# Hybrid encoder trunk: the last part of the second feed-forward in two passes by tokens

## The chip, the cores and the metric

The kernel runs on one core of one Trainium2 chip. The metric is the device time of one execution in microseconds (us); the time before is the median of three runs. The profiled execution is one more run, recorded instruction by instruction. PE is TensorE (PEld its weight loads), DVE is VectorE, ACT is ScalarE, POOL is GpSimd, SP is SyncE, which here only starts transfers.

## The reference, cut to what matters

One layer: a feed-forward, a mixer, a second feed-forward, each added to the residual `x`, and a last modulated RMSNorm. There are 640 tokens: 512 prompt tokens and 128 sample tokens (8 streams of 16), 1024 features, 2816 hidden features. The end of it is

```python
    x = x + 0.5 * g3[:, None, :] * swiglu(hn, ffn_w1[l, 1], ffn_w2[l, 1])
...
shf, scf = jnp.split(sc @ w_ada_final + b_ada_final, 2, axis=-1)
y = modulate(rmsnorm(x, final_norm_g), shf, scf)    # h * (1 + scale) + shift
```

All of it is fp32. A product is made of three products of fp32r parts: high weight by high input, high by low, low by high.

## The kernel before

**Layout.** `x` stands transposed in `xT`: eight tiles of 128 features, each over `TOK` = 640 tokens (five token tiles `c` of 128; the last, `ST`, holds the samples). Outputs are wanted by tokens, so everything that leaves has to be transposed.

**Second feed-forward.** The 22 hidden tiles are done in six parts (`PARTS`); the last part has three of them. `down(fi, part, d)` multiplies the hidden tiles of a part with the block of `ffn_w2` for feature tile `d`: 3 hidden tiles by 3 fp32r products by 2 halves of 320 tokens, 18 matmuls. For the last part the first three units stand in `first_downs` in two stretches, because the last hidden tile is late. The two halves of an accumulator lie in two PSUM banks of 2 KB per partition (`acc[0]`, `acc[1]`, `pB`, `pC` have two banks each, eight in all).

**What follows a unit `d` of the last part.** DVE adds the gated sum to `xT` (`gated_samples`, `gated_prompt` twice, `add_samples`). ACT squares the tile (line 1850), DVE adds the square to `ssum` (`add_square`). ACT (`z_prompt`) and POOL (`z_samples`) scale the tile for the last norm into `tmp`, PE turns it (`z_tile`, 5 transposes of 128 x 128 into `pB`), ACT copies it to `y_row` (`z_row`). `z_tile` for tiles 0 to 5 is put between the matmuls of later units by hand (`TURNS`).

**The end.** `mean_square(4)` takes the column means of `ssum` and of the squares of the last two tiles: 15 matmuls of 128 columns, each recorded as two passes. ACT takes the root (`rms_root`), DVE the reciprocal (`r_of`). DVE then makes ten half rows (`HALF_ROWS`, 128 x 512): `y_row * rcol + shift`, and SP sends each when it is done. `shift_row` turns the shift vectors: 8 transposes for the prompt, 8 for the samples. These and the last two `z_tile` stand behind `mean_square(4)` in PE's order. `norm_samples`, `blk` and the splitting of weights into high and low parts (ACT line 1589, DVE line 2204) are shared with the rest of the kernel.

Each engine works its own list in order; semaphores join them. A `wait_ge` holds everything behind it on that engine.

Of the kernel before, what the change touches and what calls it, by code (L numbers as in the profile page):

```python
# [7 lines left out]
ACT = mybir.ActivationFunctionType  # L8
# [76 lines left out]
def trunk_program(nc, x_prompt, x_sample, state_ssm, state_conv, c_prompt, c_sample, w_ada, b_ada, norm_g,  # L85
# [249 lines left out]

    HALF_ROWS = [(h, c) for h in range(2) for c in range(ST)] + [(h, ST) for h in range(2)]
    z_bank_of = lambda f: pC if f == KD - 1 else pB
    R_TURNS = 8
    shift_rows = acc
    sh_wide = sraw[1][:, 0:D_MODEL]  # L340
# [134 lines left out]
    def slot_as(fi, b, lo):  # L475
        kind, p, j = BLOCK[b]
        if kind != "down":
            return slot_of(fi, b, lo, WB)
        return slot_of(fi, b, lo, PARTS[p] * P).rearrange("p (k n) -> p k n", n=P)

# [76 lines left out]

    LAST_SQUARE = {1: 0, 3: 1, 4: 2}
    ADDED0 = (0, 0, KD - 1, 2 * KD - 1, 3 * KD - 2)
# [293 lines left out]
    def _(pe):  # L853
# [59 lines left out]
        def mean_square(m):  # L913

            out = pC
            j = LAST_SQUARE.get(m)
            pe.wait_ge(sq_added, ADDED0[m] + KD - (j is not None) - (m == 4))
# [3 lines left out]
            if m == 4:  # L921
                pe.wait_ge(sq_ready, m * KD - 1)
                for c in range(TT):
                    mm(out[:, c * P:(c + 1) * P], rT[:, c * P:(c + 1) * P], ones_mean[:, 0:1].broadcast_to([P, P]),
                       start=False, stop=False)
# [244 lines left out]

        TURNS = {3: {12: 0}, 4: {12: 1}, 5: {6: 2}, 6: {0: 3, 12: 4}, 7: {9: 5}}

        def z_tile(f):

            pe.wait_ge(prod_ready, 3 * KD + f + 1)
            pe.wait_ge(tms_ready, 3 * KD + f + 2)
            if f == KD - 1:
                pe.wait_ge(rms_sqrt, 5)
            else:
                wait(pe, z_rowed, f)  # L1180
            for c in range(TT):
                last = nc.tensor.transpose(z_bank_of(f)[:, c * P:(c + 1) * P], tmp[f % 2][:, c * P:(c + 1) * P],
                                           ident[:, :])
            last.then_inc(z_tr, 1)

        def shift_row(kind, fs=range(KD)):

            pe.wait_ge(down_used, 2 * len(PARTS) * KD - 1 + kind)
            for f in fs:
                v = sh_wide[:, f * P:(f + 1) * P] if kind else modc[:, 9 * KD + f, 0:1].broadcast_to([P, P])  # L1190
                last = nc.tensor.transpose(shift_rows[kind][:, f * P:(f + 1) * P], v, ident[:, :])
            last.then_inc(r_tr, 1)

        def down(fi, part, d):
# [11 lines left out]
            if halves_first:  # L1206
                ks.sort(key=lambda x: x[2])
            turned = {}
            if fi == 1 and part == len(PARTS) - 1 and d > 2:
                turned = TURNS[d]  # L1210
            for j, (k, t, h) in enumerate(ks):
                if j in turned:
                    z_tile(turned[j])
                if d == 0 and t == 0 and h == 0 and k in (0, kt - 1):
# [8 lines left out]
        def ffn(fi):  # L1223

            cols = None
            for part, kh in enumerate(PARTS):
                for p in range(PART0[part], PART0[part] + kh):
# [11 lines left out]
                    if fi == 1 and p == 0:  # L1239
                        duo_cols(DUO_GAP[1])  # L1240
                        duo_cols(DUO_GAP[1] + 1)
                if cols is None:
                    first_downs(fi, part)
# [300 lines left out]
        ffn(1)  # L1544
        mean_square(4)
        pe.wait_ge(mod_ready, 6)
        shift_row(0, range(KD // 2))
        z_tile(KD - 2)
        z_tile(KD - 1)
        shift_row(0, range(KD // 2, KD))  # L1550
        shift_row(1)


    @block.scalar
    def _(act):
# [18 lines left out]
        def blk(fi, b):  # L1574
# [245 lines left out]
        def ffn(fi, squares):  # L1820

            last_part = len(PARTS) - 1
            for part, kh in enumerate(PARTS):
# [10 lines left out]
                if part == last_part:  # L1834
                    sqrt_table()
                for d in range(KD):
# [5 lines left out]
                    if fi == 1 and d > 2:  # L1842
                        for n in {3: (0,), 4: (1, 2), 5: (3,), 6: (4,), 7: (5,)}[d]:
                            z_row(n)
                    wait(act, sq_added, squares + d - fi)
                    if d == KD - 1:
                        last_square((1, 4)[fi], x0[0] + d + 1)
                        continue
                    act.wait_ge(x_ready, x0[0] + d + 1)
                    A((rT if fi == 1 and d % 2 == 0 else sq)[:, :], tile(xT, d), ACT.Square).then_inc(sq_ready, 1)  # L1850
                    if fi == 1:
                        if d == 0:
                            act.wait_ge(mod_ready, 6)
                        z_prompt(d)
            x0[0] += KD
# [233 lines left out]
        ffn(1, ADDED0[4])  # L2089
        rms_root(4)  # L2090
        z_row(KD - 2)
        z_row(KD - 1)


    @block.vector
    def _(dve):
# [389 lines left out]
        def down(fi, part, d, q, between):  # L2486
# [6 lines left out]
            if last and d == KD - 1:  # L2493
                add_gated_by_halves((1, 4)[fi], a, q, (blk_done, b + 1), used, between)
                return
# [9 lines left out]
            else:  # L2505
                st.done(ins)

        def ffn(fi, q, sq0):

            cols = None  # L2510
            for part, kh in enumerate(PARTS):
# [15 lines left out]
                if part == len(PARTS) - 1:  # L2527
                    dve.wait_ge(ssum_zero, 1 + 2 * fi)
                for d in range(KD):
                    down(fi, part, d, q, lambda: add_square(sq0 + KD - 2 - fi, sq))  # L2530
                    if part == len(PARTS) - 1 and fi == 1:
                        if d == KD - 1:
                            dve.wait_ge(x_ready, 2 * KD + d + 1)
                            dve.wait_ge(z_tr, d - 1)
                            V.tensor_scalar(out=tmp[d % 2][:, 0:SEQ], in0=xT[:, d * TOK:d * TOK + SEQ],
                                            scalar1=modc[:, 10 * KD + d, 0:1], scalar2=None, op0=ALU.mult
                                            ).then_inc(prod_ready, 1)
                    if part == len(PARTS) - 1 and 0 < d < KD - 1:
                        if fi == 0:
                            add_square(sq0 + d - 1)  # L2540
                        elif d < KD - 2:
                            add_square(sq0 + d - 1, (rT, sq)[(d - 1) % 2])
                    for n in LOWS_BESIDE[d] if third_beside(fi, part) else (d,):
# [353 lines left out]
        ffn(1, 2, 3 * KD)  # L2897
        r_of(4)
        dve.wait_ge(rcol_ready, 5)

        def rows(c, a, b):
            return V.scalar_tensor_tensor(out=y_row[:, c, a:b], in0=y_row[:, c, a:b], scalar=rcol[:, c:c + 1],
                                          in1=shift_rows[int(c == ST)][:, a:b], op0=ALU.mult, op1=ALU.add)
        for n, (h, c) in enumerate(HALF_ROWS):
            if n == 0:
                dve.wait_ge(r_tr, R_TURNS + 1)
                dve.wait_ge(z_rowed, KD // 2)
            if n == ST:
                dve.wait_ge(r_tr, R_TURNS + 2)
                dve.wait_ge(z_rowed, KD)  # L2910
            if n == 2 * ST:
                dve.wait_ge(r_tr, R_TURNS + 3)
            rows(c, h * BANK, (h + 1) * BANK).then_inc(row_done, 1)

# [29 lines left out]
```

## Time and profile before

| | us |
|---|---|
| median of 3 runs (range) | 1439.24 (1438.28 to 1440.54) |
| time of the profiled execution | 1438.4 |
| its span, first to last instruction | 1436.8 |
| PE busy | 1419.7 (99%) |
| DVE busy | 1027.4 (72%) |
| ACT busy | 669.3 (47%) |
| POOL busy | 64.9 (5%) |

The span is what the trace covers; the run's time is 1.6 us longer. Matmuls are pipelined: one of 320 columns is recorded with some 309 ns, but starts 147 ns after the one before it. So a length of PE work is counted by starts, not by the durations of single instructions. In a timeline a line with `x5` is five instructions in a row, and its second number their common length.

### The profile page before, as it was taken

Reading aid. Unit: us, or ns where it says so; the run is one execution under the profiler, and the core shown is the slowest. Engines: PE = TensorE matmul, PEld = TensorE weight load, DVE = VectorE, ACT = ScalarE, POOL = GpSimd, SP = SyncE. Lnnn points to the kernel's source line nnn. Section 1 sums busy time; section 2 is a strip of 40 time slices with the busy share of each in tenths; the row PEclk is TensorE's granted clock in tenths of the full one; section 3 lists DMA queues with packets and bytes.
Section 4 is the critical chain, followed back from the end, with each engine's and each line's share of the span. In section 5 each row is a group of like instructions: output and inputs, shape, how many; then the busy total and the mean of one; then the engine's idle time right before and its main releaser. Section 6 shows DMA issues by size and latency. Waiting matters only on the chain.

```text
span 1436.8 us, 25703 instructions
## 1 busy us (share of the span) xinstructions
PE 1419.7 (99%) x10190; PEld 1367.3 (95%) x10190; DVE 1027.4 (72%) x1770; ACT 669.3 (47%) x1204; POOL 64.9 (5%) x109
## 2 busy tenths in 40 slices
PE   8999999999999999999999999999999999999997
PEld 6899999999999899998789999998999999999997
DVE  5887677676776776667876667557977686767776
ACT  5644425253435453666835453226525253534354
POOL 2000000000000130000100000004000000000001
PEclk9999999999999999999999999999999999999999
DMA  9752524444344612241352222443324222231222
GB/s 323 220 180 60 190 75 148 118 147 147 110 140 132 185 33 71 74 107 46 113 168 79 76 63 72 132 141 112 118 60 147 60 88 89 85 92 52 82 74 74
DMA packets 219565, 161.03 MB, mean 112 GB/s; under 512 B 6858, under 2 KB 204678, under 8 KB 219458
## 3 DMA queue, kind: packets, MB, share of 16 engines
q1 hardware_dynamic: 217490, 153.89, 36.0%
q0 software_dynamic: 1696, 5.56, 1.3%
q8 instruction: 74, 1.21, 0.4%
q14 instruction: 33, 0.27, 0.1%
q10 hardware_dynamic: 272, 0.10, 0.0%
HBM read 151.50 MB, written 8.03 MB: 111 GB/s over the span
## 4 chain that ended last, share of the span: by engine, by line
PE 93%; DVE 4%; POOL 1%; ACT 1%; DMA 1%; issue 1%; SPq 0%; DVEq 0%; ACTq 0%
PE acc L869 25%; PE pC L1098 19%; PE acc L1216 19%; PE acc L1098 15%; PE acc L1165 2%; PE pB L1014 2%; PE acc L1084 1%; PE pC L1356 1%; PE acc L1065 1%; PE pB L950 1%; PE pC L957 1%; PE pC L1491 1%; DMA x_row<-in_x_sample 1%; PE pB L1341 1%; PE acc L886 0%
## 5 line engine op out<-in xcount | busy, mean ns | idle before, releaser
L1589 ACT ACTIVATE slot<-raw 128x512 fp32r<-128x512 f32 (+1 forms) x312 | 191.0, 616 | 238.5 <-PE acc L1216 136.3
L2204 DVE TENSOR_TENSOR slot<-raw,slot 128x512 fp32r<-128x512 f32 (+1 forms) x312 | 210.3, 676 | 50.5 <-ACT slot L1589 48.1
L1216 PE MATMUL acc<-hid_hi,slot 128*128 128x320 f32 x1240 | 238.4, 310 | 0.0
L1098 PE MATMUL pC<-hn_hi,slot 128*128 128x320 f32 x960 | 227.7, 310 | 0.0
L1216 PEld LDWEIGHTS acc<-hid_hi,slot 128*128 128x128 f32 x1240 | 195.1, 188 | 2.9 <-issue 1.6
L1098 PEld LDWEIGHTS pC<-hn_hi,slot 128*128 128x128 f32 x960 | 164.4, 188 | 2.9 <-issue 2.9
L869 PE MATMUL acc<-hn_hi,whi 128*128 128x320 f32 x672 | 161.0, 321 | 0.0
L1098 PE MATMUL acc<-tT,slot 128*128 128x320 f32 x960 | 154.2, 309 | 0.3 <-DVE slot L2204 0.3
L869 PE MATMUL acc<-hn_hi,wlo 128*128 128x320 f32 x672 | 153.1, 309 | 0.0
L869 PE MATMUL acc<-hn_lo,whi 128*128 128x320 f32 x672 | 152.9, 309 | 0.0
L1098 PE MATMUL pC<-hn_lo,slot 128*128 128x320 f32 x480 | 148.2, 309 | 0.0
L1098 PEld LDWEIGHTS acc<-tT,slot 128*128 128x128 f32 x960 | 143.7, 188 | 0.6 <-DVE slot L2204 0.6
L1216 PE MATMUL acc<-hid_lo,slot 128*128 128x320 f32 x620 | 142.0, 308 | 0.0
L869 PEld LDWEIGHTS acc<-hn_hi,whi 128*128 128x128 f32 x672 | 111.8, 188 | 6.3 <-issue 5.9
L869 PEld LDWEIGHTS acc<-hn_lo,whi 128*128 128x128 f32 x672 | 112.3, 188 | 0.0
L869 PEld LDWEIGHTS acc<-hn_hi,wlo 128*128 128x128 f32 x672 | 112.2, 188 | 0.0
L1216 PEld LDWEIGHTS acc<-hid_lo,slot 128*128 128x128 f32 x620 | 103.8, 188 | 0.0
L2136 DVE TENSOR_TENSOR xadd<-acc,gate 128x128 f32<-128x128 f32 x95 | 27.6, 290 | 90.1 <-PE acc L1216 76.2
L1098 PEld LDWEIGHTS pC<-hn_lo,slot 128*128 128x128 f32 x480 | 90.1, 188 | 0.0
L2106 DVE TENSOR_TENSOR wlo<-wraw,whi 128x1024 fp32r<-128x1024 f32 x50 | 61.0, 1221 | 38.5 <-ACT whi L1569 38.0
L2130 DVE SCALAR_TENSOR_TENSOR xT<-acc,gate,xT 128x320 f32<-128x320 f32 (+1 forms) x190 | 82.6, 475 | 0.2 <-PE acc L886 0.2
L1098 PE MATMUL pC<-tT,slot 128*128 128x320 f32 x480 | 76.9, 308 | 0.0
(396 smaller groups left out, 2366.9 us busy)
## 6 DMA issues: line engine op xcount, KB each, us to landing
raw<-in_ffn_w SPq DMA_DIRECT2D x86, 512.0 KB, 5.1
sraw<-in_w_ada SPq DMA_DIRECT2D x26, 1024.0 KB, 7.6
wraw<-in_w_in SPq DMA_DIRECT2D x36, 512.0 KB, 3.8
raw<-in_ffn_w SPq DMA_DIRECT2D x16, 1024.0 KB, 5.0
ada_raw<-in_w_ada SPq DMA_DIRECT2D x8, 1024.0 KB, 11.2
wraw<-in_w_out SPq DMA_DIRECT2D x16, 512.0 KB, 4.2
raw<-in_ffn_w SPq DMA_DIRECT2D x8, 768.0 KB, 4.4
sraw<-in_w_ada_final SPq DMA_DIRECT2D x6, 1024.0 KB, 7.3
```

Source lines behind the costliest of these rows:

```text
L869: last = mm(acc[p][:, h * BANK:h * BANK + HALF], w[:, k, :], a[:, k * TOK + h * HALF:k * TOK + (h + 1) * HALF], start=(k == 0 and t == 0), ...
L950: last = nc.tensor.transpose(out[:, c * P:(c + 1) * P], src[:, c * P:(c + 1) * P], ident[:, :])
L957: last = mm(ch_rows[bank][q * QUAD:(q + 1) * QUAD, :], c_f32[:, k, :], kxn(raw, KD, ADA_COLS)[:, k, :], start=(k < P // QUAD), stop=(k >= ...
L1014: last = mm(q_rows[lane_of(duo)][q * QUAD:(q + 1) * QUAD, :], c_f32[:, k, :], kxn(duo_raw(duo, j), KD, ADA_COLS)[:, k, :], start=(kk == 0) ...
L1098: last = mm(out, w[:, kk * P:(kk + 1) * P], a, start=(first and kk == 0 and t == 0), stop=(kk == KQ - 1 and t == 2), skip_group_check=not ...
L1165: last = mm(a[h], w[t // 2][:, k, :], (hid_hi, hid_lo)[t % 2][:, k * TOK + h * HALF:k * TOK + (h + 1) * HALF], start=(k == 0 and t == 0), ...
L1216: last = mm(a[h], w[t // 2][:, k, :], (hid_hi, hid_lo)[t % 2][:, k * TOK + h * HALF:k * TOK + (h + 1) * HALF], start=(k == 0 and t == 0), ...
L1589: A(slot_as(fi, b, 0), source_of(fi, b), ACT.Copy).then_inc(blk_hi, 1)
L2106: V.tensor_tensor(out=weights(n, i, 1, w), in0=wraw[p][:, 0:w], in1=weights(n, i, 0, w).bitcast(F32), op=ALU.subtract).then_inc(wlo_done, 1)
L2130: return V.scalar_tensor_tensor(out=x[:, s:e], in0=a[s // HALF][:, p:p + e - s], scalar=gate[:, q, f * GRP:f * GRP + 1], in1=x[:, s:e], op ...
L2136: V.tensor_tensor(out=by_stream(xadd[:, SEQ:TOK]), in0=by_stream(a[1][:, SEQ - HALF:HALF]), in1=g, op=ALU.mult)
L2204: V.tensor_tensor(out=slot_as(fi, b, 1), in0=source_of(fi, b), in1=slot_as(fi, b, 0).bitcast(F32), op=ALU.subtract).then_inc(blk_lo, 1)
```

## The change

The last part of the second feed-forward gets functions of its own, `last_downs`, on PE, ACT and DVE. Tokens are worked in two passes.

- **Late pass**: tokens 256 to 639 (two prompt tiles and the samples, 384 columns) for all eight `d`, 9 matmuls of 384 columns each, every `d` in a bank of its own (`LATE_BANK`). For `d` 0 to 4 the first two hidden tiles are done for all five units, then the last hidden tile.
- **Early pass**: tokens 0 to 255 (256 columns), 9 matmuls each, two banks in turn (`EARLY_BANK`). The same weight blocks are used a second time, so the block of `d` = 7 gets a place in `hn_lo`.
- `ssum` is only added up for the late tokens. For the early tokens PE takes the column means of each unit's squares at once (`early_sum`), adding in PSUM (`sum_bank`).
- The transposes are 3 per tile for the late and 2 for the early tokens, all into one bank, `z_bank_out`.
- The root of the late tokens is taken after the late pass, the six half rows of token tiles 2, 3 and `ST` are made by DVE between the early units, and four half rows are left for the end.
- Both `shift_row` calls move ahead, into the passes.

In the order of PE (`zL`, `zE` are the transposes of late and early tokens, `sE` is `early_sum`):

```
late 0-4 (two hidden tiles), late 0-4 (last one), late 5, zL0, late 6, zL1, zL2, late 7, zL3,
early 0, zL4, early 1, zL5, zL6, shift 0, zL7, early 2, late_sums, shift 1, early 3, early 4,
zE0, sE0, zE1, sE1, early 5, zE2, sE2, early 6, zE3, sE3, zE4, sE4, early 7, zE5, sE5, zE6, sE6, sE7, zE7
```

The core of the diff:

```diff
+    SPLIT = 2 * P
+    LATE = ST - 1
+    LATE_ROWS = [(h, c) for c in (2, 3, ST) for h in range(2)]
+    HALF_ROWS = LATE_ROWS + [(h, c) for h in range(2) for c in range(2)]
+    banks = [t[:, i * BANK:(i + 1) * BANK] for t in (acc[0], acc[1], pB, pC) for i in range(2)]
+    LATE_BANK = (2, 3, 4, 5, 6, 1, 0, 7)
+    EARLY_BANK = (4, 5)
+    z_bank_out, sum_bank = banks[2], banks[3]
...
 # PE
+        def late_z(f):
+            pe.wait_ge(prod_ready, 3 * KD + f + 1)
+            pe.wait_ge(tms_ready, 3 * KD + f + 2)
...
+            wait(pe, z_rowed, f)
+            for i in range(LATE):
+                last = nc.tensor.transpose(z_bank_out[:, i * P:(i + 1) * P], tmp[f % 2][:, SPLIT + i * P:SPLIT + (i + 1) * P],
                                            ident[:, :])
             last.then_inc(z_tr, 1)
+        def early_z(f):
+            pe.wait_ge(prod_ready, 4 * KD + f + 1)
+            pe.wait_ge(z_rowed, KD + f)
+            for i in range(2):
+                last = nc.tensor.transpose(z_bank_out[:, i * P:(i + 1) * P], tmp[f % 2][:, i * P:(i + 1) * P], ident[:, :])
+            last.then_inc(z_tr, 1)
+        def early_sum(d):
+            if d == 0:
+                pe.wait_ge(rms_sqrt, 5)
+            pe.wait_ge(sq_ready, 4 * KD + d + 1)
+            for i in range(2):
+                last = mm(sum_bank[:, i * P:(i + 1) * P], (rT, sq)[d % 2][:, i * P:(i + 1) * P],
+                          ones_mean[:, 0:1].broadcast_to([P, P]), start=(d == 0 and i == 0), stop=(d == KD - 1 and i == 1))
+            last.then_inc(rms_mm if d == KD - 1 else sqhalf_ready, 1)
...
 # ACT
+        def early_row(f):
+            act.wait_ge(z_tr, KD + f + 1)
+            A(y_row[:, 0:2, f * P:(f + 1) * P], z_bank_out[:, 0:SPLIT].rearrange("p (c n) -> p c n", c=2), ACT.Copy
               ).then_inc(z_rowed, 1)
+        def early_square(d):
+            act.wait_ge(x_ready, 3 * KD + d + 1)
+            if d >= 2:
+                act.wait_ge(sqhalf_ready, len(LAST_SQUARE) + d - 1)
+            A((rT, sq)[d % 2][:, 0:SPLIT], xT[:, d * TOK:d * TOK + SPLIT], ACT.Square).then_inc(sq_ready, 1)
+        def last_downs():
+            blk(1, NB - 1)
+            act.wait_ge(mod_ready, 6)
+            for d in range(KD):
+                late_square(d)
+                if d >= 2:
+                    late_row(d - 2)
+                late_prompt(d)
+            late_row(6)
+            early_square(0)
+            early_prompt(0)
+            late_row(7)
+            early_square(1)
+            early_prompt(1)
+            token_root(LATE, 2, 4)
+            for d in range(2, KD):
+                early_square(d)
+                early_row(d - 2)
+                early_prompt(d)
+            early_row(6)
+            token_root(2, 0, 5)
+            early_row(7)
...
 # DVE
+            for d in range(KD):
+                a, x = banks[EARLY_BANK[d % 2]], tile(xT, d)
+                dve.wait_ge(x_ready, 3 * KD + d)
+                dve.wait_ge(half_done, len(LAST_SQUARE) + d + 1)
+                V.scalar_tensor_tensor(out=x[:, 0:SPLIT], in0=a[:, 0:SPLIT], scalar=gate[:, q, d * GRP:d * GRP + 1],
+                                       in1=x[:, 0:SPLIT], op0=ALU.mult, op1=ALU.add).then_inc(x_ready, 1)
+                if d == 3:
+                    token_r(2, LATE, 5)
+                    dve.wait_ge(r_tr, R_TURNS + 2)
+                    dve.wait_ge(z_rowed, KD)
+                if 3 <= d < 6:
+                    rows_of(LATE_ROWS[2 * (d - 3):2 * (d - 2)])
+            token_r(0, 2, 6)
+            dve.wait_ge(z_rowed, KD + KD // 2)
+            rows_of(HALF_ROWS[6:8])
+            dve.wait_ge(z_rowed, 2 * KD)
+            rows_of(HALF_ROWS[8:10])
```

## Rows read from the trace of the kernel before

**Rows 1.** The page: busy time of PE and DVE, share of the span.

```profile
PE 1419.7 (99%) x10190; PEld 1367.3 (95%) x10190; DVE 1027.4 (72%) x1770; ACT 669.3 (47%) x1204; POOL 64.9 (5%) x109
```

**Rows 2.** The chain that ended last, its end: start, length, what.

```profile
1398.48 3.52 PE acc L1165 x24
...
1425.26 1.13 PE pC L932 x10
...
1426.42 0.28 ACT rcol L1593
...
1426.72 0.20 DVE rcol L2216
```

**Rows 3.** Busy time by stretch: PE, PEld, DVE, ACT, POOL, granted clock, DMA.

```profile
1398.30:1426.20 27.90, 27.90 (x206) 27.67 (x205) 18.49 (x43) 17.72 (x28) 5.55 (x8) 1.00 0.00 1
```

**Rows 4.** Timeline, first unit and one set of transposes: start, length.

```profile
1398.32 0.45 PE L1165 MATMUL acc<-hid_hi,slot 128*128 128x320 f32 x2
...
1427.20 0.71 PE L1182 MATMUL pC<-ident,tmp 128*128 128x128 f32 x5
```

**Rows 5.** Groups by shape in one stretch of 1.3 us, and its timeline.

```profile
L1341 PE MATMUL pB<-wd,after_r 128*128 128x512 f32 x4 | 1.1, 394 | 0.0
646.18 1.09 PE L1341 MATMUL pB<-wd,after_r 128*128 128x512 f32 x4
```

**Rows 6.** Timeline of the end: ACT, DVE and their predecessors on PE.

```profile
1426.65 0.71 PE L1182 MATMUL pB<-ident,tmp 128*128 128x128 f32 x5
1426.94 6.67 DVE L2902 SCALAR_TENSOR_TENSOR y_row<-y_row,rcol,acc 128x512 f32<-128x512 f32 x10
1427.40 0.70 ACT L1613 ACTIVATE y_row<-pB 128x640 f32<-128x640 f32 x1 [0.71 <-PE pB L1182]
...
1428.00 0.70 ACT L1613 ACTIVATE y_row<-pC 128x640 f32<-128x640 f32 x1
```

**Rows 7.** Groups by shape, 1370 to 1440: busy, mean ns, idle before.

```profile
L2902 DVE SCALAR_TENSOR_TENSOR y_row<-y_row,rcol,acc 128x512 f32<-128x512 f32 x10 | 6.7, 741 | 0.0
L1850 ACT ACTIVATE rT<-xT 128x640 f32<-128x640 f32 x4 | 3.0, 739 | 3.4 <-DVE xT L2140 3.4
L1815 ACT ACTIVATE tmp<-pC 128x320 f32<-128x320 f32 x3 | 1.3, 438 | 2.2 <-PE pC L1098 2.2
L1620 ACT ACTIVATE sq<-xT 128x320 f32<-128x320 f32 x1 | 0.5, 470 | 0.3 <-DVE xT L2140 0.3
```

**Rows 8.** Timeline of another `mean_square`, where PE waits for a square of ACT.

```profile
976.67 0.53 PEld L932 LDWEIGHTS pC<-ones_mean,sq 128*128 128x128 f32 x4
976.78 1.52 PE L932 MATMUL pC<-ones_mean,sq 128*128 128x128 f32 x10
976.84 0.47 ACT L1620 ACTIVATE sq<-xT 128x320 f32<-128x320 f32 x1 [3.44 <-DVE xT L2140]
977.36 0.74 PEld L932 LDWEIGHTS pC<-ones_mean,sq 128*128 128x128 f32 x6 [0.17 <-ACT sq L1620]
```

**Rows 9.** Timeline of DVE in one unit of the last part.

```profile
1413.03 0.29 DVE L2136 TENSOR_TENSOR xadd<-acc,gate 128x128 f32<-128x128 f32 x1 [1.13 <-PE acc L1216]
1413.24 0.87 DVE L2130 SCALAR_TENSOR_TENSOR xT<-acc,gate,xT 128x320 f32<-128x320 f32 x2
...
1414.35 0.82 DVE L2212 TENSOR_TENSOR ssum<-ssum,sq 128x640 f32<-128x640 f32 x1
```

**Rows 10.** Busy time by stretch, as rows 3: the very end, and a busy mixed stretch.

```profile
1429.00:1430.00 1.00, 0.22 (x3) 0.00 (x0) 1.00 (x3) 0.00 (x0) 0.00 (x0) 1.00 1.03 379
...
1432.00:1433.00 1.00, 0.00 (x0) 0.00 (x0) 1.00 (x3) 0.00 (x0) 0.00 (x0) 0.50 1.03 381
716.00:720.00 4.00, 3.22 (x32) 1.53 (x28) 3.15 (x5) 2.46 (x3) 1.04 (x2) 1.00 1.01 309
```

**Rows 11.** Issues of the output transfers: count, KB, median us to landing.

```profile
out_y_prompt<-y_row SPq DMA_DIRECT2D x8, 256.0 KB, 2.2
out_y_sample<-y_row SPq DMA_DIRECT2D x2, 256.0 KB, 2.5
```

More of the change, by code:

```diff
@@ L1169, in first_downs @@
                         last.then_inc(blk_done, 1)
[L1171 to L1173 removed]
+        def late_z(f):
             pe.wait_ge(prod_ready, 3 * KD + f + 1)
             pe.wait_ge(tms_ready, 3 * KD + f + 2)
[L1177 to L1182, printed above, removed]
+            if f == 0:
+                pe.wait_ge(down_used, (2 * len(PARTS) - 1) * KD + LATE_BANK.index(2) + 1)
+            wait(pe, z_rowed, f)
+            for i in range(LATE):
+                last = nc.tensor.transpose(z_bank_out[:, i * P:(i + 1) * P], tmp[f % 2][:, SPLIT + i * P:SPLIT + (i + 1) * P],
@@ new lines, in late_sums @@
+        def late_sums():
+            pe.wait_ge(sq_added, ADDED0[4] + KD - 1)
+            for i in range(LATE):
+                mm(sum_bank[:, i * P:(i + 1) * P], ssum[:, (2 + i) * P:(3 + i) * P],
+                   ones_mean[:, 0:1].broadcast_to([P, P]), start=(i == 0), stop=False)
+            pe.wait_ge(sq_ready, 4 * KD)
+            for i in range(LATE):
+                last = mm(sum_bank[:, i * P:(i + 1) * P], sq[:, (2 + i) * P:(3 + i) * P],
+                          ones_mean[:, 0:1].broadcast_to([P, P]), start=False, stop=(i == LATE - 1))
+            last.then_inc(rms_mm, 1)
@@ new lines, in early_sum, with shift_row @@
+        def early_sum(d):
[6 more added lines that the diff above has]
+            last.then_inc(rms_mm if d == KD - 1 else sqhalf_ready, 1)
+        def shift_row(kind):
+            for f in range(KD):
@@ L1207, in down @@
                 ks.sort(key=lambda x: x[2])
[L1208 to L1213, printed above, removed]
+            for k, t, h in ks:
                 if d == 0 and t == 0 and h == 0 and k in (0, kt - 1):
@@ L1241, in ffn @@
                         duo_cols(DUO_GAP[1] + 1)
+                if fi == 1 and part == len(PARTS) - 1:
+                    last_downs()
+                    continue
                 if cols is None:
@@ L1614, in z_row, with late_square, early_prompt @@
               ).then_inc(z_rowed, 1)
+        def late_square(d):
+            wait(act, sq_added, ADDED0[4] + d - 1)
+            act.wait_ge(x_ready, 2 * KD + d + 1)
+            A((rT, sq)[d % 2][:, SPLIT:TOK], xT[:, d * TOK + SPLIT:(d + 1) * TOK], ACT.Square).then_inc(sq_ready, 1)
+        def early_prompt(f):
+            if f >= 2:
+                act.wait_ge(z_tr, KD + f - 1)
+            A(tmp[f % 2][:, 0:SPLIT], xT[:, f * TOK:f * TOK + SPLIT], ACT.Copy, scale=modc[:, 10 * KD + f, 0:1]
+              ).then_inc(prod_ready, 1)
@@ L1835, in ffn @@
                     sqrt_table()
+                if part == last_part and fi == 1:
+                    last_downs()
+                    continue
                 for d in range(KD):
@@ L2506, in down, with part_square, rows @@
                 st.done(ins)
+        def part_square(k, square, a, b, added):
+            dve.wait_ge(sq_ready, k + 1)
+            dve.wait_ge(sq_added, ADDED0[4] + added)
+            V.tensor_tensor(out=ssum[:, a:b], in0=ssum[:, a:b], in1=square[:, a:b], op=ALU.add).then_inc(sq_added, 1)
+        def rows(c, a, b):
+            return V.scalar_tensor_tensor(out=y_row[:, c, a:b], in0=y_row[:, c, a:b], scalar=rcol[:, c:c + 1],
+                                          in1=shift_rows[int(c == ST)][:, a:b], op0=ALU.mult, op1=ALU.add)
@@ L2897, in _ @@
         ffn(1, 2, 3 * KD)
[L2898 to L2913, printed above, removed]
     top.close()
```

166 lines of the change are left out of this document (117 added, 49 removed).

## The prediction

> **What bounds the kernel now.** I read the page first: PE is busy for 99% of the span [rows 1], so time can be won only by taking work off PE, or at the end, where PE has stopped. Second, the stretches: from the first matmul of the last part (1398.32 [rows 4]) to the last sum PE is busy for 27.90 of 27.90 us [rows 3]. Third, the chain that ended last: it is PE up to the sums, then the root on ACT at 1426.42, the reciprocal at 1426.72 [rows 2], and from 1426.94 the ten half rows on DVE, 6.67 us [rows 6], then the last transfer. So the end has three pieces: PE 27.9 us, then 0.20 to the root and 0.52 from root to first row, then rows of 6.67 us to 1433.6, and 3.2 us from there to 1436.8. The change shortens the third piece; the question is what it puts into the first.
>
> **Durations by start.** 24 matmuls of 320 columns take 3.52 us in the chain [rows 2]: 0.1467 each. Four of 512 columns last 1.09 us in all and one alone 0.394 [rows 5]: (1.09 - 0.394) / 3 = 0.232 from start to start. A line through both gives 0.175 for 384 columns and 0.118 for 256. Five transposes begin at 1426.65 and the next five at 1427.20 [rows 4, 6]: 0.110 each. Ten passes of the sums take 1.13 us [rows 2], near 0.111 each when not held.
>
> **PE's work up to the last sum.** Before: 144 products x 0.1467 = 21.1; 30 transposes (tiles 0 to 5) = 3.3; 15 sums in two passes, 30 x 0.111 = 3.3. Together 27.7; the trace has 27.9. After: the products are the same columns, 72 x 0.175 + 72 x 0.118 = 21.1, no change. But now stand ahead of the last sum 38 transposes of tiles (24 late, 14 early) and all 16 of the shift vectors, 54 x 0.110 = 5.9, and 22 sums (6 in `late_sums`, 16 in the `early_sum`s), 44 x 0.111 = 4.9. Together 31.9: 4.0 us more, with no wait counted. That is the price of the moves: tiles 6 and 7 and the shift vectors stood behind the sums and were hidden under the rows of DVE; now they delay the sums. Not adding up the early squares costs PE 7 more sums and takes eight additions of 256 columns off DVE, which is idle a third of the stretch (18.49 busy of 27.90 [rows 3]): it gives nothing.
>
> **The price of 256 columns.** No row has an fp32r product so narrow. It can't be shorter than a pass of the sums, which also loads 128 x 128 weights: 0.111. It can't be longer than at 320 columns, 0.147, if loading sets the pace. Against 0.118 that is -0.5 and +2.1 us over 72 products. I take 0.118, since the 320 and 512 column rows lie near a proportion to columns, and keep both ends. The Trainium skill ("TensorE: Matmul & The Clock Gate", LDWEIGHTS) has a load cost by its weight columns alone, some 107 ns for 128, and a product 2.5 ns over its columns at 2.4 GHz, 109 ns here: by that rule the split, which loads all weights twice, comes just short of being bound by loads, and the sum would be 0.65 us lower. No row here shows it.
>
> **The waits that come in.** All transposes go into one bank, `z_bank_out`. Set f+1 may start only when ACT has copied set f to `y_row`. How long PE then stands:
> - From the last transpose to the start of ACT's copy: 1427.20 to 1427.40, 0.20 [rows 4, 6].
> - The copy from PSUM lasts 438 ns for 320 columns [rows 7] and 0.70 us for 640 [rows 6], so 0.49 for 384 and 0.39 for 256.
> - From an end on ACT to PE in flow again: the square ends at 976.84 + 0.47 = 977.31, the loads resume at 977.36 [rows 8], and a matmul follows its load by 0.11 (976.67 to 976.78): 0.16.
>
> Late pass: where two sets stand with nothing between (zL1 to zL2, zL5 to zL6) PE stands 0.20 + 0.49 + 0.16 = 0.85. Twice: 1.7 us. Elsewhere an early or late unit (1.06 or 1.58) or 8 transposes (0.88) cover it.
>
> Early pass: ACT's list is square(d), copy(d-2), prompt(d). Square(d) of d >= 2 waits until `early_sum(d-2)` has read the buffer that it writes. So the copy which frees the bank is queued behind a square that waits for the sum which PE does after the transposes. From the end of a sum: 0.20, the square of 256 columns, the copy 0.39, and 0.16. The square lasts 470 ns at 320 columns and 739 at 640 [rows 7], so 0.41 at 256; the next instruction starts some 0.1 before its end (copies of 0.70 start 0.60 apart [rows 6]), so 0.32. Sum 1.07. Where an early unit stands between, its 9 x 0.118 = 1.06 covers it, for the matmul needs no more than the semaphore then (0.96). Where none stands, PE waits: zE0 sE0 to zE1, zE3 sE3 to zE4, zE5 sE5 to zE6. Three times 1.07 = 3.2 us.
>
> What is queued behind each wait is all of PE: the next sums, the next unit, and the last sum. Together 4.9 us of standing. DVE's late units are not the bound: one takes 1.32 us to the start of its `ssum` addition with 0.87 of it in two gated additions [rows 9]; with one of 256 columns (some 0.48) and `ssum` at 384 (0.55, overlapping 0.09) it is 1.39. Eight from 1404.35 give the last `x` at 1415.1 and its square at 1415.7; copy 5 on ACT waits for its transposes until 1416.0 anyway. The margin is 0.3, so a DVE unit longer by 0.2 would cost some 1.0. The square, copy and prompt of ACT take 1.26 in that 1.39. POOL's tile, the `d` = 7 block in `hn_lo` (both parts ready before unit 7, at 1411) and the waits for banks (four of them are free, as each late `d` has its own) cost nothing; the six late rows (4.0 us) on DVE lie between units where DVE would idle, and each early unit's own addition waits less than a row.
>
> **The end.** After the last sum: 0.20 + 0.52 as before, then four rows. Rows start (6.67 - 0.74) / 9 = 0.66 apart: 3 x 0.66 + 0.74 = 2.7 in place of 6.67, a gain of 4.0. The piece from the last row to the end: the transfers run at 379 GB/s with the DMA engines full from 1429 [rows 10], and the last two land after 2.5 us where the others need 2.2 [rows 11]. With six rows sent earlier this queue is shorter: I take 0.2 off (none to 0.4).
>
> **The sum.** PE 27.9 becomes 31.9 + 4.9 = 36.8: +8.9. Rows -4.0, tail -0.2. Together +4.75: a span of 1441.6 against 1436.8. The profiled execution took 1438.4, 0.8 below the median of three; I add the difference to the median: 1439.24 + 4.75 = 1444.0.
>
> **Rivals.** 0.2% of the time, 2.9 us, is about what a measurement of this kernel tells from no change.
> - *The forecast*: chance 0.52. For it: the waits follow from the order of the lists, each piece has a row. Against: copies and hand-overs of these widths aren't in the trace.
> - *Not slower: PE's stops are mostly hidden.* One mechanism: the copy is out before the square it is queued behind matters, because the sum ends earlier than I lay out. If only 0.20 + 0.39 + 0.16 less the 0.44 of the sum remains, an early stop is 0.31, three save 2.3, and the time is 1441.7; with the late stops covered too, 1440.0. It decides from 1.9 us of the 4.9 on. Against it: `early_square` names the sum as its release, and ACT works in order. Chance 0.23, of which 0.05 for faster by over 0.2%, which needs a still shorter tail and shorter sums besides.
> - *Weight loads bind at 256 columns*: 0.147 each, +2.1, 1446.1. For it: PEld is busy for 27.67 of 27.90 us [rows 3]. Against: the sums' passes load as much in 0.111. Chance 0.12.
> - *DVE binds the late pass*, as POOL and ACT run beside it: +1.0, 1445.0. Chance 0.09.
> - *The granted clock falls* to its lower level, 1.2 GHz, in the early pass. At the end it is 1.00 in 1429 to 1430, where PE stops, and 0.50 in 1432 to 1433 [rows 10]; but in a stretch with PE at 3.22 of 4.00 us it stays 1.00, and the stops here are near 1 us each. If it fell from early unit 5 on, some 7 us of PE work would double: 1451. Chance 0.04. The same page of the Trainium skill (Part 4) says that transposes don't count as busy for the clock; the 54 here stand between products, and rows 10 don't bear that out.
>
> **The numbers.** Slower by over 0.2%: 0.52 + 0.12 + 0.09 + 0.04 = 0.77. Within: 0.18. Faster: 0.05. The range takes the narrow product's upper end and half of the hidden-stop case: 1440.6 to 1446.6. The likeliest case's own range is 1442.7 to 1445.3 (five stops known to 0.1 or 0.2 each, 256 columns at 0.111 to 0.125).
>
> **What the profile after would show.** PE standing after zE0 sE0, zE3 sE3 and zE5 sE5 for about 1 us, ended by ACT's copy into `y_row`; after zL1 and zL5 for 0.85; no other stop of over 0.3. Products of 256 columns 0.118 apart. The last sum near 1435.1, 8.9 later than before. Four rows after it, 2.7 us. Wrong would be: stops under 0.4 in the early pass, which takes 2 us off, products at 0.147, or DVE ending the late pass.

## The result, and the profile after

The changed kernel takes 1444.17 us (median of 12 runs, 1442.68 to 1445.21), the kernel before 1440.47 us in its 12 runs (1438.28 to 1442.83). The ratio is 1.0028, with a 95% interval of 1.0021 to 1.0035: slower, by 3.0 to 5.0 us, with 4.0 in the middle (the two medians are 3.70 apart). The forecast was slower by 4.75 us.

The profiled execution took 1443.73 us, its span is 1442.1. The page: the busy line that answers to [rows 1], and the output transfers that answer to [rows 11].

```profile
PE 1422.7 (99%) x10204; PEld 1368.9 (95%) x10204; DVE 1025.8 (71%) x1771; ACT 673.3 (47%) x1229; POOL 63.1 (4%) x109
...
out_y_prompt<-y_row SPq DMA_DIRECT2D x8, 256.0 KB, 2.3
out_y_sample<-y_row SPq DMA_DIRECT2D x2, 256.0 KB, 2.1
```

Busy time by stretch, columns as in [rows 3]: from the first product to the end of the last sum, and two stretches of 1 us at the very end.

```profile
1399.00:1436.17 37.17, 33.04 (x244) 31.88 (x243) 21.04 (x50) 22.89 (x54) 3.84 (x8) 1.00 0.12 44
1440.00:1441.00 1.00, 0.00 (x0) 0.00 (x0) 0.00 (x0) 0.00 (x0) 0.00 (x0) 0.50 1.04 387
1441.00:1442.00 1.00, 0.00 (x0) 0.00 (x0) 0.00 (x0) 0.00 (x0) 0.00 (x0) 0.50 0.24 88
```

PE was busy for 27.90 of 27.90 us before [rows 3]. Now the stretch is 37.17 us long and PE is busy for 33.04 of it. So both terms are there: more work, and some 4 us in which nothing runs. The recorded end of a matmul lies behind the start of the next one, so the first 0.16 us of each stop still count as busy. Counted by starts, as the forecast did it, PE stands for 4.96 us and works for 32.2. The granted clock is 1.00 throughout.

The timeline shows where PE stands. Columns: start, length, engine, line, what; in brackets the idle time before, and who ended it. That idle time runs from the recorded end, so it is 0.16 or 0.17 us shorter than the stand counted by starts, which the text gives unless it says otherwise.

```profile
1399.04 0.33 PE L1233 MATMUL acc<-hid_hi,slot 128*128 128x384 f32 x1
...
1410.35 0.49 PE L1182 MATMUL acc<-ident,tmp 128*128 128x128 f32 x3
...
1410.87 0.49 ACT L1711 ACTIVATE y_row<-acc 128x384 f32<-128x384 f32 x1
1410.98 0.40 POOL L852 TENSOR_TENSOR tmp<-xT,modc 128x128 f32<-128x128 f32 x1 [1.38 <-PE acc L1182]
...
1411.51 0.52 PE L1182 MATMUL acc<-ident,tmp 128*128 128x128 f32 x3 [0.67 <-POOL tmp L852]
...
1417.38 0.52 PE L1182 MATMUL acc<-ident,tmp 128*128 128x128 f32 x3 [0.67 <-POOL tmp L852]
...
1424.19 1.41 DVE L2662 SCALAR_TENSOR_TENSOR y_row<-y_row,rcol,acc 128x512 f32<-128x512 f32 x2
...
1424.34 0.38 PE L1191 MATMUL acc<-ident,tmp 128*128 128x128 f32 x2
...
1424.56 0.61 PE L1212 MATMUL acc<-ones_mean,rT 128*128 128x128 f32 x4
...
1425.27 0.42 ACT L1738 ACTIVATE rT<-xT 128x256 f32<-128x256 f32 x1 [3.44 <-PE acc L1212]
1425.51 0.48 DVE L2697 SCALAR_TENSOR_TENSOR xT<-pB,gate,xT 128x256 f32<-128x256 f32 x1
1425.59 0.36 ACT L1730 ACTIVATE y_row<-acc 128x256 f32<-128x256 f32 x1
...
1426.10 0.41 PE L1191 MATMUL acc<-ident,tmp 128*128 128x128 f32 x2 [0.93 <-ACT y_row L1730]
...
1431.46 0.41 PE L1191 MATMUL acc<-ident,tmp 128*128 128x128 f32 x2 [0.93 <-ACT y_row L1730]
...
1435.04 0.41 PE L1191 MATMUL acc<-ident,tmp 128*128 128x128 f32 x2 [0.93 <-ACT y_row L1730]
...
1435.73 0.61 PE L1212 MATMUL acc<-ones_mean,sq 128*128 128x128 f32 x4
...
1436.38 0.26 ACT L1743 ACTIVATE rcol<-acc,eps_t 128x2 f32<-128x2 f32 x1 [0.51 <-PE acc L1212]
...
1436.87 2.72 DVE L2662 SCALAR_TENSOR_TENSOR y_row<-y_row,rcol,acc 128x512 f32<-128x512 f32 x4
```

**Early stops.** The four passes of `early_sum(0)` begin at 1424.56 and take 4 x 0.111, to 1425.00; zE1 begins at 1426.10. That is a stand of 1.10. In between, in ACT's order: the square from 1425.27, and behind it the copy from 1425.59, which ends at 1425.95 and lets PE go on 0.15 later. The pieces are 0.27 + 0.32 + 0.36 + 0.15, where the forecast had 0.20 + 0.32 + 0.39 + 0.16. It happens three times, ahead of zE1, zE4 and zE6.

**Late stops.** zL1 begins at 1410.35 and takes 3 x 0.11, to 1410.68; zL2 begins at 1411.51: 0.83, and once more before zL6. Here the profile names POOL as the one who ended it. But the POOL instruction at 1410.98 is a tile that PE doesn't need yet. ACT's copy, which ends at 1410.87 + 0.49 = 1411.36, fits with its hand-over of 0.15. The experiment with a bank more settles it.

The chain that ended last runs through all three early stops; a part of it, with the last one:

```profile
1432.32 1.06 PE pB L1233 x9
...
1434.20 0.42 ACT sq L1738
1434.62 0.28 ACT y_row L1730
```

Its first line also has the price that no row of before showed: nine products of 256 columns in 1.06 us, 0.118 each.

**Count from the first product.** No code ahead of the last part differs, and yet the first product of the last part begins at 1398.32 before [rows 4] and at 1399.04 after, and anywhere from 1397.87 to 1401.95 in the profiles below. So two profiles are compared from that product on, and what a kernel is worth is taken from the ratios.

| | before | after | difference | forecast |
|---|---|---|---|---|
| first product to root | 28.10 | 37.34 | +9.24 | +8.9 |
| root to end of span | 10.38 | 5.72 | -4.66 | -4.2 |
| together | 38.48 | 43.06 | +4.58 | +4.75 |

### The profile page after: what moved, and what is told of

Its sections match the earlier page's. It is cut to its first block, busy times and chain, and to the rows that moved or that the text cites. A ratio compares the mean times of both kernels' runs of the same rounds, so it can differ in the third digit from the quotient of the medians.

```text
span 1442.1 us, 25783 instructions
## 1 busy us (share of the span) xinstructions
PE 1422.7 (99%) x10204; PEld 1368.9 (95%) x10204; DVE 1025.8 (71%) x1771; ACT 673.3 (47%) x1229; POOL 63.1 (4%) x109
## 4 chain that ended last, share of the span: by engine, by line
PE 92%; DVE 3%; ACT 1%; SPq 1%; POOL 1%; DMA 1%; issue 1%; DVEq 0%; POOLq 0%; ACTq 0%
PE acc L877 25%; PE pC L1101 19%; PE acc L1316 18%; PE acc L1101 15%; PE pB L1017 2%; PE acc L1168 2%; PE acc L1087 1%; PE pC L1459 1%; DMA ada_raw<-in_w_ada 1%; PE pB L1233 1%; PE acc L1068 1%; PE pB L953 1%; PE pC L1594 1%; PE pB L1444 1%; PE acc L894 0%
## 5 line engine op out<-in xcount | busy, mean ns | idle before, releaser
L1316 PE MATMUL acc<-hid_hi,slot 128*128 128x320 f32 x1180 | 225.2, 309 | 0.0
L1316 PEld LDWEIGHTS acc<-hid_hi,slot 128*128 128x128 f32 x1180 | 185.4, 188 | 2.9 <-issue 2.1
L1316 PE MATMUL acc<-hid_lo,slot 128*128 128x320 f32 x590 | 134.7, 308 | 0.0
L1316 PEld LDWEIGHTS acc<-hid_lo,slot 128*128 128x128 f32 x590 | 98.7, 188 | 0.0
L1101 PE MATMUL acc<-hn_hi,slot 128*128 128x320 f32 x320 | 76.9, 309 | 0.0
```

The costliest lines, as they stand in the source:

```text
L1101: last = mm(out, w[:, kk * P:(kk + 1) * P], a, start=(first and kk == 0 and t == 0), stop=(kk == KQ - 1 and t == 2), skip_group_check=not ...
L1316: last = mm(a[h], w[t // 2][:, k, :], (hid_hi, hid_lo)[t % 2][:, k * TOK + h * HALF:k * TOK + (h + 1) * HALF], start=(k == 0 and t == 0), ...
```

## Experiments

"To root" is from the first product of the last part to the root of the last tokens, from the profile. Each ratio is to runs of the kernel before on the same chip, side by side with the kernel's own.

| kernel | ratio to before | 95% interval | to root | to end |
|---|---|---|---|---|
| changed kernel | 1.0028 | 1.0021 to 1.0035 | 37.34 | 43.06 |
| copy first | 1.0014 | 1.0005 to 1.0023 | 34.66 | 40.39 |
| early bank | 1.0007 | 0.9998 to 1.0016 | 34.76 | 40.49 |
| late bank | 1.0020 | 1.0011 to 1.0029 | 36.19 | 41.95 |
| both banks | 1.0003 | 0.9994 to 1.0012 | 33.46 | 39.16 |
| sum alone | 1.0012 | 1.0003 to 1.0021 | 35.01 | 40.75 |
| both banks, DVE sums | 1.0002 | 0.9993 to 1.0011 | 33.17 | 38.88 |
| combined | 0.9992 | 0.9983 to 1.0001 | 31.82 | 37.57 |
| before, work moved | 1.0008 | 0.9999 to 1.0017 | 29.52 | 40.61 |
| rows first | 0.9975 | 0.9964 to 0.9985 | 30.14 | 35.83 |
| rows first, sums at once | 0.9996 | 0.9987 to 1.0005 | 32.81 | 38.52 |

**1. The copy ahead of the square on ACT (e1_copy_first).** It tests the claimed cause of the early stops by order alone.

```diff
             for d in range(2, KD):
+                early_row(d - 2)
                 early_square(d)
-                early_row(d - 2)
                 early_prompt(d)
```

> Edit: in ACT's early list the copy into y_row of tile d-2 stands before the square of d instead of behind it. Theory (PE's three early stops of 1.10 us are the chain sum, square, copy): a stop becomes 0.20 + 0.37 + 0.16 less the 0.44 of the sum, about 0.3 us; three save 2.3 us, span about 1439.8 against 1442.1 of the changed kernel, ratio to before about 1.0012. Rival (the stops are set by the scaled tile or the buffers of the squares, and the copy only happens to be last): the stop stays over 0.9 us and the span within 0.5 of 1442.1.

Measured 1442.29 us, ratio 1.0014. The timeline at the place of the first early stop:

```profile
1426.23 0.61 PE L1212 MATMUL acc<-ones_mean,rT 128*128 128x128 f32 x4
1426.43 0.38 ACT L1730 ACTIVATE y_row<-acc 128x256 f32<-128x256 f32 x1 [2.93 <-PE acc L1191]
...
1426.93 0.42 ACT L1738 ACTIVATE rT<-xT 128x256 f32<-128x256 f32 x1
1426.96 0.41 PE L1191 MATMUL acc<-ident,tmp 128*128 128x128 f32 x2
```

The copy now runs while PE takes the sums, and the stand is 1426.96 - 1426.67 = 0.29 in place of 1.10. The other two are 0.29 as well. Three times 0.81 is 2.4; the root comes 2.7 us sooner. The cause is shown: the stop is the square that waits for the sum and has the copy behind it.

**2. A second bank for the early transposes (e2_early_bank).** The same stops, taken on from PE's side. Odd tiles go to the bank that holds half of the samples' shift vectors, so the samples' late rows are made first. The transposes and ACT's copy then use `early_out(f)`.

```diff
-    LATE_ROWS = [(h, c) for c in (2, 3, ST) for h in range(2)]
+    LATE_ROWS = [(h, c) for c in (ST, 2, 3) for h in range(2)]
...
+    early_out = lambda f: banks[(2, 6)[f % 2]]
...
-            pe.wait_ge(z_rowed, KD + f)
+            pe.wait_ge(z_rowed, KD + max(f - 1, 0))
+            if f == 1:
+                pe.wait_ge(row_done, 2)
```

> Edit: the early transposes go into two PSUM banks in turn (bank 2 and the first of pC, free after the samples' rows, which DVE makes first), so set f+1 waits for the copy of set f-1. Theory: the stop before the second set stays at 0.7 us (it waits for the samples' rows), the two others vanish; the last sum comes 2.3 to 2.5 us earlier, span about 1439.7, ratio to before about 1.0012. Rival (the square waiting for the sum is what counts, not the bank): PE stops for as long before the next sum instead, span within 0.5 of 1442.1.

Measured 1441.19 us, ratio 1.0007, somewhat under the expectation. The root comes 2.6 us sooner. One early stop is left, a new one of 0.73 (0.57 in the bracket): PE waits for DVE's first two rows to free the bank. The expectation had 0.7 for it.

```profile
1427.20 0.41 PE L1194 MATMUL pC<-ident,tmp 128*128 128x128 f32 x2 [0.57 <-DVE y_row L2665]
```

**3. A second bank for the late transposes (e3_late_bank).** It decides who ends the late stops.

```diff
+    late_out = lambda f: banks[2 + f % 2]
...
-            wait(pe, z_rowed, f)
+            wait(pe, z_rowed, f - 1)
...
         def late_sums():
 
+            pe.wait_ge(z_rowed, KD)
```

> Edit: the late transposes go into two banks in turn (bank 3 is free until the late sums). Theory (the two late stops of 0.83 us are PE waiting for ACT's copy out of the one bank): zL1-zL2 has no stop, zL5-zL6 one of 0.3 us because ACT then scales tile 6 just in time; 1.25 us less, span about 1440.85, ratio to before about 1.0020. Rival (POOL's scaling of the samples, which the profile names as releaser, binds): both stops stay at 0.8, span 1442.1.

Measured 1442.28 us, ratio 1.0020. The timeline, around zL1 and zL2, and around zL5 and zL6:

```profile
1409.65 0.82 PE L1185 MATMUL acc<-ident,tmp 128*128 128x128 f32 x6
...
1410.23 0.42 PE L1237 MATMUL pC<-hid_hi,hn_lo 128*128 128x384 f32 x1
...
1410.29 0.41 POOL L853 TENSOR_TENSOR tmp<-xT,modc 128x128 f32<-128x128 f32 x1 [1.38 <-PE acc L1185]
...
1414.67 1.05 PE L1185 MATMUL acc<-ident,tmp 128*128 128x128 f32 x6
1415.56 1.04 PE L1224 MATMUL acc<-ident,modc 128*128 128x128 f32 x8
```

Six transposes stand in a row. POOL's instruction begins at 1410.29, when the product behind them has already started, so POOL released none of them; in the changed kernel it was the copy. The two stops were 1.66 us; the root comes 1.15 sooner, since the second pair takes 0.89 where 6 x 0.11 would do, and there are gaps of some 0.1 before zL7 and in `late_sums`.

**4. Both banks (e4_both_banks).** Both edits together: do they add up?

> Edit: e2 and e3 together. Theory: the savings add, 3.5 us, PE stands for about 1.5 us of the 5.0 in all, span about 1438.6, ratio to before about 1.0004 (within 0.2% of before): the change without its stops is then no gain, since the longer PE work ahead of the last sum (4 us) uses up the four rows' worth that the end gives back. Rival (the stops are only a part and other losses show up): span above 1440.

Measured 1440.69 us, ratio 1.0003. The root comes 3.88 us sooner than in the changed kernel; the edits alone gave 2.58 and 1.15. They add up: 3.73, and 3.88 measured. But the kernel is only even with the one before: what is left is the added work of PE against the rows saved. One stop of over 0.3 us is left, of 0.73:

```profile
1423.65 0.41 PE L1197 MATMUL pC<-ident,tmp 128*128 128x128 f32 x2 [0.57 <-DVE y_row L2669]
```

**5. The sums at once undone alone (e8_sum_alone).** DVE adds up the early squares 0 to 5; PE takes means of `ssum` and of squares 6 and 7. All else is as in the changed kernel.

```diff
+            if d < KD - 2:
+                return
+            if d == KD - 2:
...
+                    mm(sum_bank[:, i * P:(i + 1) * P], ssum[:, i * P:(i + 1) * P],
+                       ones_mean[:, 0:1].broadcast_to([P, P]), start=(i == 0), stop=False)
...
-                act.wait_ge(sqhalf_ready, len(LAST_SQUARE) + d - 1)
+                act.wait_ge(sq_added, ADDED0[4] + LATE_ADDED + d - 1)
...
+                if 0 < d < KD - 1:
+                    part_square(4 * KD + d - 1, (rT, sq)[(d - 1) % 2], 0, SPLIT, LATE_ADDED + d - 1)
```

> The changed kernel with one part undone: the early squares 0 to 5 are added up by DVE and TensorE takes 12 passes in place of 32. Everything else, the single bank for transposes and the order of ACT's list included, stays. My account: 2.2 us less TensorE work ahead of the root; the square of d + 2 now waits for DVE's addition and no longer for TensorE's sum, but the copy that frees the bank is still queued behind it, so three early stops of about 0.9 to 1.4 each stay or grow because the passes of the sums between sets of transposes no longer cover part of them: root 36 us after the first product instead of 37.3, ratio to the kernel before 1.0017 to 1.0022. Rival (the sums at once were the main cost of the change): ratio 1.0012 or less, root at 35.1 or earlier.

Measured 1441.53 us, ratio 1.0012, root at 35.01: the rival's numbers, not mine. I had expected the stops to grow by some 0.9 us (2.2 of work saved, and the root only 1.3 sooner). The timeline:

```profile
1428.21 0.41 PE L1192 MATMUL acc<-ident,tmp 128*128 128x128 f32 x2 [0.56 <-ACT y_row L1738]
...
1432.15 0.41 PE L1192 MATMUL acc<-ident,tmp 128*128 128x128 f32 x2 [1.04 <-ACT y_row L1738]
...
1433.37 0.42 ACT L1746 ACTIVATE rT<-xT 128x256 f32<-128x256 f32 x1 [0.96 <-DVE xT L2705]
...
1434.20 0.41 PE L1192 MATMUL acc<-ident,tmp 128*128 128x128 f32 x2 [0.61 <-ACT y_row L1738]
...
1435.17 0.41 PE L1192 MATMUL acc<-ident,tmp 128*128 128x128 f32 x2 [0.57 <-ACT y_row L1738]
```

Four stands of 0.73, 1.19, 0.77 and 0.75 (from the end of the transposes or products before) make 3.44 in place of 3.30. The saving stays whole: 20 passes x 0.111 = 2.2, of 2.33 measured. The copy no longer waits for a sum of PE, only for DVE and the square. Taking the column means at once is the largest single piece of work that the change put in PE's way, at 2.2 us; the five stops together cost more than twice that.

**6. Both banks and the sum by DVE (e5_dve_sum).** The edit of 5 on the kernel of 4.

> The kernel with a bank more for both kinds of transposes (the kernel of the run before this one), and the early squares of units 0 to 5 are added up by DVE again; TensorE takes the column means of that sum and of the squares 6 and 7 only: 12 passes instead of 32, so 20 x 0.111 = 2.2 us less TensorE work ahead of the root. Theory A (the sums that stand in the way are a plain cost of TensorE): the root comes 2.2 us earlier, 31.3 us after the first product instead of 33.46, and the ratio to the kernel before is 0.9988. Theory B (DVE is the price: six additions of some 0.4 us and six late rows of 0.66 us now lie between the early units, an addition waits behind two rows of 1.3 us, and the square of d + 2 waits for it): TensorE stands where it flowed, 1.5 to 2.5 us in all, and the root comes at 33.0 to 33.9 us; ratio 1.0003. I hold B for likelier.

Measured 1439.55 us, ratio 1.0002, root at 33.17, as theory B had it. Of the 2.2 us only 0.3 arrives. The timeline, at both stops:

```profile
1426.27 0.41 PE L1198 MATMUL pC<-ident,tmp 128*128 128x128 f32 x2 [1.35 <-DVE y_row L2677]
...
1428.81 1.40 DVE L2677 SCALAR_TENSOR_TENSOR y_row<-y_row,rcol,acc 128x512 f32<-128x512 f32 x2
...
1430.13 0.48 DVE L2712 SCALAR_TENSOR_TENSOR xT<-pB,gate,xT 128x256 f32<-128x256 f32 x1
...
1430.64 0.42 ACT L1753 ACTIVATE rT<-xT 128x256 f32<-128x256 f32 x1 [0.61 <-DVE xT L2712]
...
1431.78 0.44 PE L1198 MATMUL acc<-ident,tmp 128*128 128x128 f32 x2 [1.05 <-ACT tmp L1739]
```

The stop for DVE's rows grows from 0.57 to 1.35 in the bracket. A second one of 1.05 appears before zE6: ACT's square had waited 0.61 for an addition that stood behind two rows on DVE, and the scaling which PE needs stands behind this square and a copy. By starts the stops grow by 2.0 in all. With PE's stops gone, DVE is the next in line.

**7. The rows spread, the last late square by DVE too (e6_combined).** The edit against the kernel of 6; `late_sums` then takes the means of `ssum` alone.

```diff
+    ROWS_TO = (0, 2, 3, 3, 4, 6)
...
+                if d == 1:
+                    part_square(4 * KD - 1, sq, SPLIT, TOK, KD - 1)
...
-                if 3 <= d < 6:
-                    rows_of(LATE_ROWS[2 * (d - 3):2 * (d - 2)])
+                if d >= 3:
+                    rows_of(LATE_ROWS[ROWS_TO[d - 3]:ROWS_TO[d - 2]])
```

> As the kernel with DVE adding up the early squares, and two things more: the last late square is added by DVE too (late_sums 6 passes in place of 12, 0.7 us less on TensorE), and the six late rows are spread over the early units as 2, 1, 0, 1, 2 instead of 2, 2, 2, so that fewer additions wait behind a pair of rows. Theory A (TensorE's work ahead of the root is what counts once the stops are gone): 2.9 us less than with the banks alone, root 30.6 us after the first product, ratio 0.9984, faster than the kernel before. Theory B (the rows on DVE still hold the squares up): root at 32 us or later, ratio 0.9994 or above.

Measured 1438.10 us, ratio 0.9992, between the two theories: root at 31.82, 1.6 us sooner than with the banks alone, of 2.9 in work. The timeline has what is missing. By starts PE stands 1.48 before zE1, where the kernel of 4 has 0.73, and 0.51 before zE6, where it has none. That is 1.26 us more, of the 1.3 that are missing.

```profile
1422.06 1.41 DVE L2674 SCALAR_TENSOR_TENSOR y_row<-y_row,rcol,pC 128x512 f32<-128x512 f32 x2
...
1423.61 0.41 PE L1199 MATMUL pC<-ident,tmp 128*128 128x128 f32 x2 [1.32 <-DVE y_row L2674]
...
1428.44 0.44 PE L1199 MATMUL acc<-ident,tmp 128*128 128x128 f32 x2 [0.35 <-ACT tmp L1736]
```

**8. The kernel before, with work moved ahead of its sums (e7_before_moved).** It prices one term alone.

```diff
-        mean_square(4)
         pe.wait_ge(mod_ready, 6)
         shift_row(0, range(KD // 2))
+        shift_row(0, range(KD // 2, KD))
         z_tile(KD - 2)
+        mean_square(4)
         z_tile(KD - 1)
-        shift_row(0, range(KD // 2, KD))
         shift_row(1)
```

> The kernel before, with the 8 transposes of the prompt's shift vectors and the 5 of tile 6 moved ahead of the column means on TensorE. It prices one term alone: work that is moved from behind the last sum to ahead of it. My account: 13 transposes x 0.110 = 1.4 us later root, nothing back, ratio 1.0010, and the root 29.5 us after the first product instead of 28.1. Rival: the moved work fills slack that the last squares leave, and the time stays within 0.5 us (ratio 1.0003 or less).

Measured 1441.40 us, ratio 1.0008; the interval reaches down to 0.9999, so the time alone tells little. The trace tells it: root 29.52 after the first product against 28.10, which is +1.42 for 13 x 0.110 = 1.43. The shift vectors of the prompt and the set of tile 6, now ahead of the sums:

```profile
1425.55 1.03 PE L1191 MATMUL acc<-ident,modc 128*128 128x128 f32 x8
...
1426.42 0.71 PE L1182 MATMUL pB<-ident,tmp 128*128 128x128 f32 x5
```

**9. The first two late rows ahead of unit 3 (e9_rows_first).** In the trace of 7 the root of the late tokens and the shift vectors are there by 1420, while DVE waits for unit 3. The rows of the samples go first, and zE6 goes behind two of the sums.

```diff
-    ROWS_TO = (0, 2, 3, 3, 4, 6)
+    ROWS_TO = (2, 2, 2, 3, 4, 6)
...
+                if d == 3:
+                    token_r(2, LATE, 5)
+                    dve.wait_ge(r_tr, R_TURNS + 2)
+                    dve.wait_ge(z_rowed, KD)
+                    rows_of(LATE_ROWS[0:2])
                 dve.wait_ge(x_ready, 3 * KD + d)
...
             early_sum(5)
+            early_sum(6)
             early_z(6)
-            early_sum(6)
             early_sum(7)
```

> The combined kernel with its last two stops taken on. In its trace TensorE stands 1.32 us before the second set of early transposes, until DVE's first two rows (the samples) have freed the bank of the samples' shift vectors, though root, shift vectors and y_row are there before unit 3's addition; so DVE makes these two rows ahead of the addition of unit 3, and the other four rows are spread 0, 1, 1, 2 over units 4 to 7. And it stands 0.35 before the transposes of tile 6; so these go behind the sums of ssum and square 6. Theory (stops are a plain cost, and each that goes comes off the time): the root 30.2 us after the first product in place of 31.82, ratio to the kernel before 0.9980. Rival (the rows ahead of unit 3's addition hold back early unit 5, whose bank it frees, so that the stop only moves): root 31.3 or later, ratio 0.9988 to 0.9992.

Measured 1436.21 us (1435.45 to 1438.25), ratio 0.9975, interval 0.9964 to 0.9985: faster than the kernel before by 3.6 us and than the changed one by some 7.6. The two traces, from the first product on, have less against the kernel before: 38.48 - 35.83 = 2.65. The root comes at 30.14, as worked out. The two edits were not run apart; in the trace both stands are gone. Its timeline at both former stops, and the windows:

```profile
1419.47 1.41 DVE L2674 SCALAR_TENSOR_TENSOR y_row<-y_row,rcol,pC 128x512 f32<-128x512 f32 x2 [0.45 <-PE pC L1232]
...
1421.35 0.38 PE L1199 MATMUL acc<-ident,tmp 128*128 128x128 f32 x2
1421.57 0.38 PE L1199 MATMUL pC<-ident,tmp 128*128 128x128 f32 x2
...
1427.01 0.38 PE L1199 MATMUL acc<-ident,tmp 128*128 128x128 f32 x2
...
1427.23 0.71 PE L1223 MATMUL acc<-ones_mean,sq 128*128 128x128 f32 x4
```

```profile
1397.80:1427.80 30.00, 29.95 (x218) 28.97 (x216) 23.18 (x57) 21.69 (x54) 4.53 (x8) 1.00 0.10 36
```

Against [rows 3] the stretch is 2 us longer and as full; the four rows and the shorter end give back more than that.

**10. The same with the sums at once (e10_rows_first_sums_at_once).**

It is the kernel of 4 with the late rows placed as in 9, and with the order of PE as it was.

> The same placing of the six late rows, with TensorE taking the column means of each early square at once, as in the changed kernel: 32 passes instead of 12 for the early tokens and 12 instead of 6 in late_sums, 26 x 0.111 = 2.9 us more TensorE work than the kernel it stands beside, and no addition of early squares on DVE. Theory (with the stops gone the sums at once cost their full length): root 32.8 to 33.1 us after the first product, ratio 0.9998 to 1.0001. Rival (the sums fill time in which TensorE would wait for ACT and DVE): root at 31.5 or earlier, ratio within 0.0007 of the kernel it stands beside.

Measured 1439.58 us, ratio 0.9996 against 0.9975 on the same chip: 3.0 us, where 26 passes make 2.9. The root comes 2.67 later. With the stops gone, the sums at once cost their full length.

## Why the prediction was right

The mechanism was the forecast's, with its places. That the forecast time, 1444.0, and the measured one, 1444.17, agree to 0.2 us is luck in part: the kernel before came out at 1440.47 over 12 runs, 1.2 above the median of three that the forecast started from, and the change cost some 1 us less than forecast. Point by point:

- **PE's work up to the last sum, 31.9.** The stretch of 37.13 us less the stops of 4.96 is 32.2. Products of 384 columns were 0.174 to 0.175 apart, of 256 columns 0.118 to 0.119. The other 0.27 is mostly in small gaps where sums and transposes alternate. The moved work is a plain cost (experiment 8), and so are the sums at once (5, 10). That the sums at once give nothing was right; the prediction counted them at 1.6 us (14 more passes). The real alternative, with DVE adding as before, saves 20 passes here.
- **The late stops, 2 x 0.85:** 2 x 0.83, and the copy is their cause (3).
- **The early stops, 3 x 1.07:** 3 x 1.10, by the mechanism named (1, 2).
- **Wrong, without effect here:** "each early unit's own addition waits less than a row". Unit 4's last product ends at 1424.22 + 0.28 = 1424.50, its addition begins at 1425.51, behind two rows: 1.0 us, where a row takes 0.66 to 0.74. PE stood at zE1 meanwhile. In 6 a wait of this kind costs time.
- **The end.** From root to first row 0.49 (0.52 before), four rows in 2.72 (2.7). The piece from the last row to the end was mis-sized: I took 0.2 off 3.2, none to 0.4 as bounds. It is 1442.1 - 1439.59 = 2.5, 0.7 off.
- **The sum.** +4.58 by the traces against +4.75. By the ratio it is +4.0 with an interval of 3.0 to 5.0; the forecast lies in its upper part. By the traces the two largest misses, +0.3 on PE and -0.5 at the end, cancel in part.
- **The rival that would end on the other side** (early stops near 0.31) is what the kernel becomes when the copy goes first: 0.29 each. It fails for the reason given against it, the wait of `early_square` for the sum.
- **Loads as the bound at 256 columns** would need 0.147; it is 0.118 to 0.119. The line through two widths was the better guess. The Trainium skill ("TensorE: Matmul & The Clock Gate", Back-to-back issue gap) gives a single matmul on its own its columns at 2.4 GHz and 2.5 ns more; for 256 columns that makes an estimate of 0.109. The trace lies 8 to 9% above that.
- **DVE as the bound of the late pass:** its units are 1.38 to 1.40 apart, as worked out (the last 1.59), and PE waits only for the copies there. Not seen. DVE does become the next limit once the stops are gone and it adds the squares as well (6, 7).
- **The clock:** 1.00 in the whole stretch, 54 transposes and stands of 1.10 included.

What stays open: how much of the difference between +4.58 by two traces and +4.0 by the ratio (+3.70 by the medians) is chance of single profiles. The tail of a ten-row end alone was 3.2 in one profile and 3.9 in another; no run tests what sets it.

## What to carry to other kernels

Where PE is full, work moved ahead of the last instruction that others wait for costs the number of its instructions times the interval between their starts, and a split that shortens what comes behind must save more than this: count both before asking about waits. When work is cut finer, follow each single buffer round its loop through every engine's list: a copy that frees PE's bank must not stand behind an instruction that waits for PE. Two more banks, the sums given back to DVE and another order of a few instructions turned a loss of 2.8 per mille into a gain of 2.5.

## What the runs showed of the hardware

- With four rows left at the end, the time from the last row's end to the end of the span is 2.48 to 2.55 us in all ten profiles; with ten rows it was 3.2 and 3.9. At ten rows the DMA engines are full from 1429 on [rows 10]. With four they are full at 387 GB/s in 1440 to 1441 too, and at 0.24 in the next microsecond. A shorter queue behind the last row would fit this; no run tests it.
- The last part begins up to 4.1 us apart (1397.87 to 1401.95) in profiles of kernels that do the same work ahead of it. A difference of two spans is worth little below that.
- The releaser that the profile names can be another one than the true: at the late stops it names a POOL instruction which PE doesn't need. A wait for several semaphores is tested by freeing one of them.
